# Keeping the last token block's gates on chip for 80 of 128 expert groups in a two-layer diffusion step with product-key experts

## The reference

```python
def _layer(x, mods, params, attend):
    sh1, sc1, gt1, sh2, sc2, gt2 = mods          # silu(cond) @ w_ada + b_ada
    h = _rmsnorm(x, g1) * (1 + sc1) + sh1
    a_in, a_b, a_c, p_in, q, k, v = jnp.split(h @ w_in_l, IN_SPLITS, axis=-1)
    y = jnp.concatenate([_short_conv(...), _multi_pool(...), attention], axis=-1)
    x = x + gt1 * (y @ w_out_l)
    h = _rmsnorm(x, g2) * (1 + sc2) + sh2
    return x + gt2 * _peer(h, wq_l, sk_l, u_l, v_l)

def _peer(x, w_q, sub_keys, u, v):               # per token 8 heads x 16 of 16384 experts
    q = (xt @ w_q).reshape(T, PEER_HEADS, 2, PEER_HALF)
    sv, si = lax.top_k(einsum(q, sub_keys), 16)  # then top 16 of the 16 x 16 sums
    experts, gates = i1 * 128 + i2, softmax(top)
    h = gelu(einsum('tkd,td->tk', u[experts], x))
    return einsum('tk,tkd->td', gates * h, v[experts])
```

## Time and profile before

| what | before |
|---|---|
| median of 3 runs | 2676.51 us (2668.55 to 2679.03) |
| the profiled execution's own time | 2672.81 us |
| its span | 2671.0 us |
| mean granted TensorE clock | 0.979 |
| TensorE matmul, busy | 2488.9 us (93%) |
| VectorE, busy | 2032.5 us (76%) |
| ScalarE, busy | 1162.2 us (44%) |
| GpSimd, busy | 991.8 us (37%) |

### The profile page before, as it was taken

One profiled execution on the slowest core, in us unless ns is written; L12 is line 12 of the kernel. 1 busy time (PEld: TensorE's weight loads), 2 busy tenths in 40 slices (PEclk: granted clock), 3 DMA queues, 4 the chain that ended last, 5 costly groups with the idle time before them and its releaser, 6 DMA issues.

```text
span 2671.0 us, 44784 instructions
## 1 busy us (share of the span) xinstructions
PE 2488.9 (93%) x16674; PEld 2408.7 (90%) x16674; DVE 2032.5 (76%) x3708; ACT 1162.2 (44%) x1933; POOL 991.8 (37%) x667
## 2 busy tenths in 40 slices
PE   6998998889999899999999899898999999999997
PEld 6978998889999889999999799798999999999997
DVE  3544687889987499999965467789898955777764
ACT  3444543335466333333344545333363743333332
POOL 0012007878783123333020210378888801222200
PEclk8999999999999999999999999999999999999998
DMA  7395259986966999999843633699869589999871
GB/s 311 118 303 180 89 185 367 353 280 146 235 161 197 329 403 391 381 394 377 306 166 120 148 114 133 239 345 359 236 169 231 131 278 360 349 336 353 330 281 68
DMA packets 303733, 684.60 MB, mean 256 GB/s; under 512 B 87696, under 2 KB 219664, under 8 KB 258512
## 3 DMA queue, kind: packets, MB, share of 16 engines
q1 hardware_dynamic: 218880, 496.32, 53.5%
q0 software_dynamic: 84688, 186.16, 22.5%
HBM read 595.36 MB, written 86.64 MB: 255 GB/s over the span
## 4 chain that ended last, share of the span: by engine, by line
PE 53%; DVE 23%; issue 11%; DMA 7%; ACT 3%; POOL 1%; SPq 1%; DVEq 0%; POOLq 0%; ACTq 0%
PE ps L1096 19%; PE ps L1037 16%; PE ps L869 10%; DVE u_lo L1756 5%; DMA act_scratch<-act_h 4%; DVE u_rows_s L1768 2%; DVE acc_s L2021 2%; DVE v_lo L1996 2%; DVE mod_p L2062 2%; DMA act<-act_scratch 2%; PE ps L891 1%; PE ps L1061 1%; ACT u_hi L1318 1%; DVE w L2005 1%; PE ps L976 1%
## 5 line engine op out<-in xcount | busy, mean ns | idle before, releaser
L1037 PE MATMUL ps<-h_lo,u_hi 128*128 128x320 f32 x2048 | 648.7, 317 | 70.6 <-DVE u_lo L1756 61.3
L1096 PE MATMUL ps<-w_hi,v_lo 128*128 128x320 f32 (+1 forms) x2048 | 642.8, 314 | 40.8 <-DVE v_lo L1996 36.4
L1096 PE MATMUL ps<-w_hi,v_hi 128*128 128x320 f32 x2048 | 636.5, 311 | 0.0
L1096 PE MATMUL ps<-w_lo,v_hi 128*128 128x320 f32 x2048 | 636.5, 311 | 0.0
L1037 PE MATMUL ps<-h_hi,u_hi 128*128 128x320 f32 x2048 | 635.9, 311 | 0.0
L1037 PE MATMUL ps<-h_hi,u_lo 128*128 128x320 f32 x2048 | 635.8, 310 | 0.0
L751 POOL DMA_INDIRECT gate_scratch<-scat x256 | 514.3, 2009 | 87.7 <-issue 75.3
L1388 ACT CAST v_hi<-wring 128x1024 fp32r<-128x1024 f32 x256 | 268.5, 1049 | 510.1 <-PE ps L1096 504.3
L1037 PEld LDWEIGHTS ps<-h_lo,u_hi 128*128 128x128 f32 x2048 | 387.2, 189 | 95.3 <-DVE u_lo L1756 80.0
L1096 PEld LDWEIGHTS ps<-w_hi,v_lo 128*128 128x128 f32 x2048 | 387.9, 189 | 52.5 <-issue 34.5
L1996 DVE TENSOR_TENSOR v_lo<-wring,v_hi 128x1024 fp32r<-128x1024 f32 x256 | 313.0, 1223 | 156.4 <-ACT v_hi L1388 156.3
(11 more groups left out here) (275 smaller groups left out, 3548.6 us busy)
## 6 DMA issues: line engine op xcount, KB each, us to landing
wring<-in_u_t_dram SPq DMA_DIRECT2D x128, 1024.0 KB
wring<-in_v_t_dram SPq DMA_DIRECT2D x128, 1024.0 KB
act_scratch<-act_h SPq DMA_DIRECT2D x256, 160.0 KB
gate<-gate_scratch SPq DMA_DIRECT2D x64, 640.0 KB
act<-act_scratch SPq DMA_DIRECT2D x64, 640.0 KB
wring<-in_w_ada_dram SPq DMA_DIRECT2D x24, 1024.0 KB
mod_w<-in_w_mod_dram POOLq DMA_DIRECT2D x24, 1024.0 KB, 7.8
wring<-in_w_in_dram SPq DMA_DIRECT2D x20, 1024.0 KB
```

The costliest lines, as they stand in the source:

```text
L1037: last = nc.tensor.matmul(ps[:, 6 + s % 2, 0:TD], u[:, s % 2, k], hx[:, k, 0:TD], start=(k == 0 and n == 0), stop=(k == KC - 1 and n == 2))
L1096: last = nc.tensor.matmul(ps[:, half * (KC // 2) + c, cols], v[:, of % 4, d], w[:, group * G + of, cols], start=(opening and k == 0), stop ...
```

## The change

The last token block is now block 0 (ORDER is (2, 1, 0)), so that its tokens are the first 128 columns. SyncE stores only SENT = 3 of the 8 pieces of its gates; those of the 80 key groups from KEPT = 48 on stay in `g_all`, and VectorE multiplies the first 128 columns by `g_all` and the other 192 by `gate2`, of which SyncE then loads only the 192. To let `g_all` live on, `mod_w` and `c_b` are put where the hidden stage's `h_hi`, `u_hi`, `u_lo` and `act_h` lie, `w_lo` and `gate2` lose the last 64 columns, and `acc_s` and `mod_p` share a smaller place. The waits follow: GpSimd waits for three pieces instead of eight before `sel`, and for all stores of `act_h` instead of the first ones before `c_b`; ScalarE waits for the last modulation dot before it writes `u_hi` for the next layer; SyncE no longer waits for pieces 3 to 7. Modulation starts 10 units earlier (MOD_UNIT 16 for 26), the rows of `v` 4 units earlier (V_FIRST 20 for 24). Apart from that the 64 dots of the hidden stage start in step 6 instead of step 2 and are spread evenly to step 55, and GpSimd's wait for the zero fill moves from before the squares to before the first scatter.

```diff
...
-MOD_UNIT = 26
+MOD_UNIT = 16
...
-ORDER = (2, 0, 1)
+ORDER = (2, 1, 0)
...
-ROUTE_DOTS = tuple((s >= 2) + (s % 6 == 5) + (s == 2) for s in range(ROUTE_LEN[1]))
+DOTS_FROM = 6
+ROUTE_DOTS = tuple((s + 1 - DOTS_FROM) * SLOTS // (ROUTE_LEN[1] - DOTS_FROM) - max(s - DOTS_FROM, 0) * SLOTS // (ROUTE_LEN[1] - DOTS_FROM)
+                   if s >= DOTS_FROM else 0 for s in range(ROUTE_LEN[1]))
...
-V_FIRST, V_EVERY, V_AHEAD = 24, 3, 10
+V_FIRST, V_EVERY, V_AHEAD = 20, 3, 10
...
+SENT = 3
+KEPT = SENT * NK // PIECES
...
-    w_lo = at("w_lo", [P, 2 * G, T], F32R)
+    w_lo = at("w_lo", [P, 2 * G, TD], F32R)
     w32 = at("w32", [P, 2, T])
-    gate2 = at("gate2", [P, 2, G, T])
+    gate2 = at("gate2", [P, 2, G, TD])
...
+    place[0] = split_at + 24 * D
+    mod_w = at("mod_w", [P, 2, 2, D])
     c_b = at("c_b", [P, 2, D])
-    mod_w = at("mod_w", [P, 2, 2, D])
-    mod_p = at("mod_p", [P, D])
+    assert place[0] <= hidden_end
...
-            def load_ga(g, buf):
+            def load_ga(g, buf, first=0):
...
-                for dst, src in ((gate2, gate_dram), (act2, act_dram)):
-                    sp.dma_start(dst[:, buf, :, 0:TD], src[bass.ds(g * G, G), :, 0:TD].rearrange("b e t -> e b t")) \
+                for dst, src, at_ in ((gate2, gate_dram, first), (act2, act_dram, 0)):
+                    sp.dma_start(dst[:, buf, :, at_:TD], src[bass.ds(g * G, G), :, at_:TD].rearrange("b e t -> e b t")) \
...
                 group_loads(2 + n, n)
-                for piece in ((3, 4), (5, 6, 7))[n]:
-                    store_gates(TB - 1, piece)
-            for sig in g_st[3:]:
-                sp.wait_ge(sig.sem, sig.at(l, 16 * GT))
-                sp.sem_inc(sp_passed.sem, 1)
...
-            with sp.Fori(2, NG // 2) as i:
+            with sp.Fori(2, KEPT // (2 * G)) as i:
                 for n in range(2):
                     group_loads(i * 2 + n, n)
+            with sp.Fori(KEPT // (2 * G), NG // 2) as i:
+                for n in range(2):
+                    group_loads(i * 2 + n, n, first=P)
...
-            pool.wait_ge(nought_st.sem, nought_st.at(l, 32 * PIECES))
-            pool.sem_inc(pool_passed.sem, 1)
             pool.wait_ge(o_evac.sem, o_evac.at(l, NU))
...
+            pool.wait_ge(nought_st.sem, nought_st.at(l, 32 * PIECES))
+            pool.sem_inc(pool_passed.sem, 1)
             for half in range(2):
                 cells_in_two(half)
...
-            for sig in g_st:
+            for sig in g_st[:SENT]:
                 pool.wait_ge(sig.sem, sig.at(l, 16 * GT))
...
                 for sig in act_st:
-                    pool.wait_ge(sig.sem, sig.at(0, 16 * (2 * G // AR)))
+                    pool.wait_ge(sig.sem, sig.at(0, 16 * (NB // AR)))
...
+                    if n == 9:
+                        act.wait_ge(mod_sum.sem, 4 * N_MOD)
...
-                V.tensor_tensor(w32[:, :, 0:TD], act2[:, buf, b:b + 2, 0:TD], gate2[:, buf, b:b + 2, 0:TD], ALU.mult).then_inc(w32_rdy.sem, 2)
+                first = 0
+                if B >= KEPT:
+                    first = P
+                    V.tensor_tensor(w32[:, :, 0:P], act2[:, buf, b:b + 2, 0:P], g_all[:, B:B + 2], ALU.mult)
+                V.tensor_tensor(w32[:, :, first:TD], act2[:, buf, b:b + 2, first:TD], gate2[:, buf, b:b + 2, first:TD], ALU.mult) \
+                    .then_inc(w32_rdy.sem, 2)
...
```

More of the change, by code:

```diff
@@ L240, in build @@
     w_hi = at("w_hi", [P, 2 * G, T], F32R)
-    w_lo = at("w_lo", [P, 2 * G, T], F32R)
+    w_lo = at("w_lo", [P, 2 * G, TD], F32R)
     w32 = at("w32", [P, 2, T])
-    gate2 = at("gate2", [P, 2, G, T])
+    gate2 = at("gate2", [P, 2, G, TD])
     act2 = at("act2", [P, 2, G, T], offset=h_at)
-    acc_at = place[0]
     acc_s = at("acc_s", [P, D])
+    mod_p = at("mod_p", [P, D])
     sel = at("sel", [P, NS])
-    diag_r = at("diag_r", [P, TB, P])
-    place[0] = acc_at + 4 * TB * D
+    assert place[0] <= g_all_at + 4 * P * KEPT
+    place[0] = split_at + 24 * D
+    mod_w = at("mod_w", [P, 2, 2, D])
     c_b = at("c_b", [P, 2, D])
-    mod_w = at("mod_w", [P, 2, 2, D])
-    mod_p = at("mod_p", [P, D])
+    assert place[0] <= hidden_end
+    diag_r = at("diag_r", [P, TB, P], offset=hidden_end)
     scat = at("scat", [P, 2, 2, PICKS2], offset=hidden_end)
@@ L366, in build @@
     tq_evac = S("tq_evac", NQ, credit=2)
-    g_st = [S(f"g_st{i}", 16 * GT, credit=16) for i in range(PIECES)]
+    g_st = [S(f"g_st{i}", 16 * (GT if i < SENT else GT - 1), credit=16) for i in range(PIECES)]
     nought_rdy = S("nought_rdy", 0)
@@ L601, in _, with group_loads @@
             store_acts(NB // (2 * WR), 4)
-            def group_loads(g, n, ga=True):
-                if ga:
-                    sp.wait_ge(w32_rdy.sem, l * NB + (g - 1) * G)
-                    load_ga(g, n)
+            def group_loads(g, n, first=0):
+                sp.wait_ge(w32_rdy.sem, l * NB + (g - 1) * G)
+                load_ga(g, n, first)
                 for half in range(2):
@@ L2027, in _ @@
                     v_lo_step(0, 0)
+            dve.wait_ge(gq_evac.sem, gq_evac.at(l, NQ))
+            dve.wait_ge(tq_evac.sem, tq_evac.at(l, NQ))
             dve.wait_ge(ga_ld[0].sem, ga_ld[0].at(l, 32))
```

## The result

The changed kernel takes **2657.91 us** (median of 8 runs, 2647.09 to 2663.11) against 2676.76 for the kernel before (8 runs, 2668.55 to 2680.49). The ratio is 0.9931, 95% interval 0.9916 to 0.9946: 18.9 us faster, where 39.7 were forecast. The profiled execution took 2663.11 us, the longest of its runs; single runs of the two kernels lie up to 11 us from their medians, so small differences between two traces are to be read with care.

What follows compares the result with a forecast made beforehand. TensorE, busy 2488.9 of 2671.0 us, was taken as near its floor. Terms −8.9 − 12.3 − 13.5 + 2.5 − 7.5 = −39.7 gave 2633.1, put at 2637 us on the runs' median; range 2620 to 2663.

Steps and rivals of the forecast that it cites:

- Term 1: Layer 0, before GpSimd adds the squares: moving the zero fill's wait leaves 0.6 us of TensorE's wait; −8.9 us.
- Term 2: Hidden stage, both layers: dots starting in step 6 no longer stall steps 2 to 6, some given back later; −12.3 us.
- rival C: Dots' stretch of the hidden stage: bound by VectorE and the gathers, gain returns as waits; 12.3 lost, 2649 us, chance 0.15.
- rival G: Follow-up run moving second dots to short steps: gathers and stores in flight hold the stretch; no gain, ratio 0.993.
- Rival A: Hidden stage: the dots pay in full, with no give-back in steps 6 to 55; −8.2 more, 2629 us, chance 0.10.
- Terms 3 and 5: Start of the V (expert output) stages: wait for fifth group's loads goes; −13.5 us layer 0, −7.5 us layer 1.
- term 4: V stage: split multiply for 40 pairs of key groups a layer costs +2.5 us in layer 0, hidden in layer 1.
- Term 6: The rest, such as 10 MB of gate stores and 10 MB of loads saved, mid V stages: worth nothing.
- B: V stage start, layer 0: stall only changes its name, c_b, mod_w and rows late; 13.5 lost, 2650 us, chance 0.12.
- D: Hidden stage: late rows delay GpSimd's scatter-adds, SyncE waits before the first gate load; slower, 2703 us, chance 0.04.

Runs made afterwards that it cites:

- a_olddots: The changed kernel with the dots' old schedule (first dots in step 2): 2649.61 us, ratio 0.9906 to the kernel before.
- b_newdots: The kernel before with the dots' new schedule alone: 2688.38 us, ratio 1.0055.
- a_paced: The changed kernel with row fetches 4 to 15 of the first burst waiting for hidden steps: 2657.39 us, ratio 0.9935 to the kernel before.
- a_vonly: The changed kernel with both the old dots and the old place of the zero fill's wait: 2655.62 us, ratio 0.9933 to the kernel before.
- b_latewait: The kernel before with only SyncE's wait for pieces 3 to 7 moved from the fifth to the thirteenth group: 2675.49 us, ratio 1.0009.
- a_vonly_stores: a_vonly with the five stores put back and SyncE waiting for them only ahead of the thirteenth group: 2683.05 us, ratio 1.0032 to the kernel before.

## Why the prediction was right and wrong

- **Term 1 (−8.9, measured −4.4 in the trace, −3.7 alone).** The wait left as said. The step that failed is "0.6 of TensorE's wait is left": it took the adds' duration of before, when VectorE stood idle. Beside a working VectorE they take 2.4 us more, and TensorE waits 2.3. The 1.5 us for the clock did not show either: the wait shrank by 5.7 us and the hidden stage begins only 4.4 sooner.
- **Term 2 (−12.3, measured +7 to +15, by `a_olddots` and `b_newdots`).** This is the failed term. Of rival C's mechanism the half that names VectorE happened, beyond its price of 0, and the half that names the gathers did not (rival G fell). The step at fault is "I charge 0.6 of the 6.8". It took a mean over 49 steps, 3.5 us of VectorE in 4.0, for slack that any dot can use. The slack is in the short steps; the order put 4 of 14 second dots into steps of 4.1 to 4.5 us of other work, and one into step 55. From step 6 to step 58 the traces show 5.5 us more in layer 0 and 17.7 in layer 1 (`b_newdots`: 11.7 and 18.1), so mostly more than the whole of the 6.8. The traces with well placed dots from step 6 show the opposite end: 209.5 to 214.8 us, where the old order has 211.9 to 217.3, so the same six dots cost nothing there. Rival A's own "against" had named this, a second dot that falls on long top-k work; the prediction used it against A only and gave it no price of its own. Beside it layer 0 lost 6.3 us of its 10.8 to ScalarE's wait, which the prediction had not looked for: once the dots no longer wait for rows, the stores issued among the rows are late next (`a_paced`, with the rows issued later, has 14.6 us there).
- **Terms 3 and 5 (−13.5 and −7.5; with term 4 −18.5, measured −18 in `a_vonly`).** Sizes right, cause half right. The prediction gave the stall to SyncE's wait, which alone is worth nothing (1.0009); GpSimd's wait on the same stores keeps most of it in `b_latewait`, and the stores themselves keep it in `a_vonly_stores`, where both waits are out of the way. That c_b would be the next thing late was read rightly, and is what `b_latewait` ran into; in the change it is on time. Term 6 put the 10 MB of stores at nothing in the middle of the V stages, but five of them stand at their start and carry 27 us.
- **Term 4 (+2.5, measured +4, 0 to 9; in the trace about +3 in layer 0 and nothing in layer 1).** Right, and so is its price for a pair, 0.07 in the rows. The +4.8 that the prediction put beside it does not fit these rows.
- **Rivals.** A did not occur with the change's order of dots (the well placed ones show it), and B not at all; D neither: the last row is issued at 574.7 us and GpSimd's last add at 824.7 is 35 us ahead of the first gate load. D's "14 double-dot steps instead of 8" counts to step 55; up to step 43, which it speaks of, there are 10 instead of 6.

The terms measured alone sum to −18 − 3.7 + 14.7 = −7, the whole to −18.9: the dots seem to cost less in the changed kernel (6.7 us between `a_olddots` and it) than in the kernel before (14.7). With intervals of 4 to 6 us on each number this is at the edge of what can be told, and why it should be so is open.

## What to carry to other kernels

An engine that is 87% busy has no slack to hand out until it is known in which steps the slack lies: take its own time step by step, and place movable work where that time plus the work stays under the step of the engine that bounds. A risk that a rival names wants a price before it is set aside. When a queue of transfers stands ahead of a stall, ask who else waits for the same transfers and what issuing them costs; removing one wait of three that end together gained nothing here. And a duration read while the neighbouring engine stood idle is not the duration after an edit that lets both run.
